# A two-layer encoder step on one core: residual stream kept feature by token, projections in split fp32r passes

## The chip, the core and the metric

The kernel runs on one core of one Trainium2 chip. The metric is device time in microseconds (us), as the median of the runs shown. Engines are named as in the profile: PE multiplies matrices (PEld is its loading of weights), DVE, ACT and POOL are the vector, scalar and GpSimd engines, SP issues loads from memory. PSUM is the banked memory into which PE adds up products.

## What is computed

320 tokens (256 of a prompt, 64 of running streams; in tiles of 128, 128 and 64) go through two layers of width 1024. The reference, cut to what matters:

```python
xn = rmsnorm(x, g_mix)
qa, ka, va, ga, ra, bb, cb, hb, qc, kc, vc = split_cols(xn @ w_in)
lg = jax.nn.log_sigmoid(ga @ w_g2 + b_g2) / GATE_TAU
o_a, s1 = gla_recurrence(s0, q, k, v, lg)
y_a = rmsnorm(o_a, g_gla) * jax.nn.silu(ra)
y_b, buf1 = short_conv(bb, cb, hb, w_conv, buf0)
o_c = diff_prompt(qd, kd, vd, lam)
y_c = rmsnorm(o_c, g_sub) * (1.0 - lam_init)
x = x + jnp.concatenate([y_a, y_b, y_c], axis=-1) @ w_out
x = x + ffn(rmsnorm(x, g_ffn))
```

w_in has 3088 columns: qa and ka 192 each, va, ra, qc, kc and vc 384 each, ga 16, bb, cb and hb 256 each. qd and kd are qc and kc after a norm per head and the rotary turn (rope). The ffn is dense SwiGLU (width 2816) in layer 0 and the top 2 of 8 SwiGLU experts (width 3584) in layer 1. Everything is fp32 in and out.

## The kernel before

Each engine runs one list of instructions, written out by hand, and waits on semaphores; the order on each engine is the order of the code. Weights come through a ring of three slots of 2 MB, filled by SP in the order of `UNITS`. PSUM banks are rings with a list of jobs each (A two banks, D three, S two, O one); a job can start when the job that had its bank before is read out.

One layer is mixed like this. x lies in rows, token by feature. `norm_tile` (L1473): ACT squares a tile, POOL takes the root, DVE scales it (L1001), PE transposes it (L1450), and ACT or DVE copies it with the gain into `xT`. Then PE projects. `tokens` and `token_tile` (L1508, L1500) make rows of qk, kc, qc, vc, va and ra, three token tiles of 384 columns each, as plain fp32 matmuls with `xT` as the stationary operand; `features` (L1493) makes ga and the blocks of bb, cb and hb feature by token. All matmuls are recorded at the helper `mm` (L1447), all transposes at `tr` (L1450). Gate logits go through DVE (L1050), the decays through ACT and DVE (L750 to L752, L1052 to L1061), rope through DVE (L1037 and L1080 to L1083), `heads_T` turns q and k, and ACT copies them. A loop over 12 heads (three tiles of four heads) follows, with the rest of the projections, the recurrence and the attention woven in. `project` (L1711) multiplies the mixed rows by w_out, in fp32, first the gated rows (three blocks of 128 features), then the convolution and the attention.

The dense FFN works otherwise: `CUTS` are pieces of 128 weight columns (8 x 128 x 128), each split by ACT into a high part in fp32r (`cut_hi`, L885) and by DVE into the rest (`cut_lo`, L1277), three cuts deep; `three` (L1751) multiplies in three fp32r passes: high by high, low weight by high x, high weight by low x. The experts work the same way on pieces of 2048 elements per partition (`split_hi` L916, `split_lo` L1351; matmuls L1869 to L1880).

Of the kernel before, what the change touches and what calls it, by code (L numbers as in the profile page):

```python
# [15 lines left out]
F32 = mybir.dt.float32  # L17
FR = mybir.dt.float32r
# [7 lines left out]
P = 128  # L26
# [38 lines left out]

RING = 3
SLOT = KB * 512
# [3 lines left out]
for _l in range(DEPTH):  # L71
    UNITS += [("qk", _l), ("kc", _l), ("qc", _l), ("vc", _l), ("va", _l), ("ra", _l), ("bc", _l), ("hb", _l),
              ("wo", _l, 0), ("wo", _l, 1)]
    if _l == 0:
        for _j in range((FB + 3) // 4):
            UNITS += [("g", _j), ("u", _j)]
        UNITS += [("d", _c, _j) for _c in range(2) for _j in range((FB + 7) // 8)]
UNIT = {u: n for n, u in enumerate(UNITS)}


def is_dense(u):
    return u[0] in ("g", "u", "d")


def plain_units(n):

    return sum(not is_dense(u) for u in UNITS[:n])

CUT = KB * P
CUTS = []
for _f in range(FB):
    CUTS += [(("g", _f // 4), "g", _f), (("u", _f // 4), "u", _f)]
for _c in range(2):
    CUTS += [(("d", _c, _m // 4), "d", (_c, _m)) for _m in range(FB // 2)]
CR = 3
LAST_CUT = {u: q for q, (u, _k, _w) in enumerate(CUTS)}
DOWN0 = 2 * FB  # L100
HALF = FB // 2
DOWN_BANKS = [[("A", 4 * _c), ("D", 4 * _c + 2), ("A", 4 * _c + 1), ("D", 4 * _c + 3)] for _c in range(2)]
UE = 3 * FC

PIECE = SLOT // 2
# [16 lines left out]
JOBS_A, JOBS_D, JOBS_S, JOBS_O = [], [], [], []  # L122


def _norm_jobs(i):
    for t in range(NT):
        JOBS_A.append(("xt", i, t))
        JOBS_D.append(("xt", i, t))


JOBS_A += [("par",), ("bcast", 0)]
JOBS_D += [("bcast", 1)]
for _l in range(DEPTH):
    _norm_jobs(2 * _l)
    JOBS_A += [("ga", _l)] + [("qk", _l, t) for t in range(NT)] + [("qkt", _l, t) for t in range(NT)]
    JOBS_A += [("pk", _l)] + [("kt", _l, t) for t in range(NT)] + [("vc", _l, t) for t in range(NT)]
    JOBS_A += [("qt", _l, t) for t in range(NT)] + [("va", _l, t) for t in range(NT)] + [("kd", _l, t) for t in range(NT)]
    JOBS_A += [("at", _l, 0), ("at", _l, 1), ("bb", _l, 0), ("at", _l, 2), ("bb", _l, 1), ("at", _l, 3), ("at", _l, 4)]
    JOBS_A += [("cb", _l, 0), ("at", _l, 5), ("cb", _l, 1)] + [("at", _l, n) for n in range(6, HEADS)]
    JOBS_A += [("ya", _l, t) for t in range(NT)] + [("wo", _l, 0), ("wo", _l, 1)]  # L140
    JOBS_D += [("gl", _l, 0), ("gl", _l, 1)]
    JOBS_D += [("kc", _l, t) for t in range(NT)] + [("qc", _l, t) for t in range(NT)]
    JOBS_D += [("ra", _l, 0), ("ra", _l, 1)] + [("att", _l, t) for t in range(NT)]
    JOBS_D += [("U", _l, 0), ("U", _l, 1), ("U", _l, 2), ("ra", _l, 2), ("U", _l, 3), ("U", _l, 4)]
    JOBS_D += [("oa", _l, t) for t in range(NT)] + [("hb", _l, 0), ("hb", _l, 1)]
    JOBS_D += [("wo", _l, t) for t in range(NT)]
    JOBS_S += [("s", _l, n) for n in range(HEADS)] + [("yc", _l, t) for t in range(NT)]
    JOBS_O += [("oc", _l, t) for t in range(NT)] + [("wo", _l, 2)]
    _norm_jobs(2 * _l + 1)
    if _l == 0:  # L150
        for _f in range(FB):
            JOBS_A.append(("g", _f))
            JOBS_D.append(("u", _f))
        JOBS_A += [("dT", _o) for _o in (0, 1, 4, 5)]
        JOBS_D += [("dT", _o) for _o in (2, 3, 6, 7)]
        for t in range(NT):
            JOBS_A.append(("dn", t))
            JOBS_D.append(("dn", t))
JOBS_D += [("lg", t) for t in range(NT)] + [("rk", t) for t in range(NT)] + [("cnt",), ("idx0",), ("idx",)]


class PsumRing:


    def __init__(self, banks, jobs, full, free):
        self.banks, self.full, self.free = banks, full, free
        self.n = {j: i for i, j in enumerate(jobs)}
        self.count = len(jobs)
# [36 lines left out]
def build(nc, A, O):  # L205
# [5 lines left out]
    with ExitStack() as ctx:  # L211
# [7 lines left out]
        A_full, A_free = sem("A_full"), sem("A_free")  # L219
        D_full, D_free = sem("D_full"), sem("D_free")  # L220
        S_full, S_free = sem("S_full"), sem("S_free")
        O_full, O_free = sem("O_full"), sem("O_free")
        RA_ = PsumRing(banks[0:2], JOBS_A, A_full, A_free)
        RO_ = PsumRing(banks[2:3], JOBS_O, O_full, O_free)

        RD_ = PsumRing([banks[3 + (i - len(JOBS_D) + 1) % 3] for i in range(3)], JOBS_D, D_full, D_free)
        RS_ = PsumRing(banks[6:8], JOBS_S, S_full, S_free)


        x = sb("x", [P, NT, D])  # L230
# [1718 lines left out]
```

## Time and profile before

| what | us |
|---|---|
| median of three runs (1794.09 to 1795.8) | 1794.45 |
| the profiled execution, own time | 1799.02 |
| its span on the core | 1797.2 |
| PE busy, of the span | 1705.6 (95%) |
| DVE busy | 1167.9 (65%) |
| ACT busy | 921.8 (51%) |
| POOL busy | 119.7 (7%) |

The profile is of one execution. The span is that of the core's instructions; the execution's own time is 1.8 us longer. Shares over the whole span mix stages: some 230 us of mixing a layer, 237 us of dense FFN, 976 us of experts. What holds a stage up is read from that stage.

### The profile page before, as it was taken

The numbers are of one execution on the slowest core, as the hardware profiler recorded it, in microseconds if no ns is written. First come the engines' busy times: TensorE is split into PE (matmuls) and PEld (weight loads), VectorE is DVE, ScalarE is ACT, GpSimd is POOL, SyncE is SP. The second block draws the span as 40 slices with busy tenths as digits, with TensorE's granted clock in tenths as the row PEclk, the third lists the DMA queues.
The fourth block names the chain that finished last, engine by engine and source line by source line (L and its number), as shares of the span: only waits on it lengthen the run. The fifth ranks groups of instructions, "written<-read, shape, count | busy, mean of one in ns | idle before, by whom it ended". The sixth has DMA issues, their size and how long they took to land.

```text
span 1797.2 us, 20002 instructions
## 1 busy us (share of the span) xinstructions
PE 1705.6 (95%) x7922; PEld 1305.3 (73%) x7922; DVE 1167.9 (65%) x1157; ACT 921.8 (51%) x975; POOL 119.7 (7%) x168
## 2 busy tenths in 40 slices
PE   5999979999999999879999999999999999999994
PEld 3456639999965566468878878888788788888883
DVE  2415524554325145168888888888888888888884
ACT  2312223333223112137777777777777777777772
POOL 4300200000012002010000000000000000000001
PEclk9999989999999989969999999999999999999997
DMA  5321227525413211079999999999999999999993
GB/s 171 101 97 47 97 103 272 184 75 200 141 58 116 82 48 51 29 286 363 360 368 379 368 372 369 358 386 365 359 386 361 370 377 359 378 373 358 385 365 100
DMA packets 202878, 450.02 MB, mean 250 GB/s; under 512 B 9634, under 2 KB 34928, under 8 KB 202784
## 3 DMA queue, kind: packets, MB, share of 16 engines
q1 hardware_dynamic: 187776, 420.63, 64.8%
q10 hardware_dynamic: 10944, 17.13, 2.7%
q0 software_dynamic: 4064, 10.96, 1.9%
q8 instruction: 64, 1.05, 0.2%
q14 instruction: 30, 0.25, 0.0%
HBM read 431.22 MB, written 17.47 MB: 250 GB/s over the span
## 4 chain that ended last, share of the span: by engine, by line
PE 90%; DVE 6%; ACT 2%; issue 1%; DMA 1%; ACTq 0%; POOL 0%; POOLq 0%; DVEq 0%
PE bank L1447 37%; PE bank L1869 12%; PE bank L1870 12%; PE bank L1871 12%; PE bank L1877 5%; PE bank L1880 5%; PE bank L1878 5%; PE bank L1450 2%; DVE split_lo L1351 2%; PE bank L1889 1%; DVE xgT_lo L1375 1%; ACT split_hi L916 1%; DMA raw<-expert_rows,pos 0%; DVE G L1342 0%; DVE xhat L1001 0%
## 5 line engine op out<-in xcount | busy, mean ns | idle before, releaser
L1351 DVE TENSOR_TENSOR split_lo<-raw,split_hi 128x2048 fp32r<-128x2048 f32 x336 | 768.2, 2291 | 133.7 <-ACT split_hi L916 133.7
L916 ACT CAST split_hi<-raw 128x2048 fp32r<-128x2048 f32 x336 | 641.2, 1913 | 268.9 <-PE bank L1871 169.0
L1869 PE MATMUL bank<-split_hi,xgT_hi 128*128 128x512 f32 x896 | 359.4, 401 | 6.0 <-DVE xgT_lo L1375 6.0
L1870 PE MATMUL bank<-split_lo,xgT_hi 128*128 128x512 f32 x896 | 355.8, 397 | 0.0
L1871 PE MATMUL bank<-split_hi,xgT_lo 128*128 128x512 f32 x896 | 355.7, 397 | 0.0
L1447 PE MATMUL bank<-ring,xT 128*128 128x384 f32 (+3 forms) x720 | 258.9, 516 | 5.3 <-DVE t L1037 3.4
L1447 PEld LDWEIGHTS bank<-ring,xT 128*128 128x128 f32 (+1 forms) x720 | 123.1, 174 | 130.3 <-issue 83.4
L1869 PEld LDWEIGHTS bank<-split_hi,xgT_hi 128*128 128x128 f32 x896 | 169.3, 189 | 45.8 <-DVE xgT_lo L1375 6.4
L1871 PEld LDWEIGHTS bank<-split_hi,xgT_lo 128*128 128x128 f32 x896 | 169.1, 189 | 41.1
L1870 PEld LDWEIGHTS bank<-split_lo,xgT_hi 128*128 128x128 f32 x896 | 169.5, 189 | 39.3
L1877 PE MATMUL bank<-split_hi,hmT_hi 128*128 128x512 f32 x448 | 179.3, 400 | 3.0 <-DVE split_lo L1351 3.0
L1878 PE MATMUL bank<-split_lo,hmT_hi 128*128 128x512 f32 x448 | 175.8, 392 | 0.0
L1277 DVE TENSOR_TENSOR cut_lo<-ring,cut_hi 128x1024 fp32r<-128x1024 f32 x66 | 80.7, 1225 | 120.2 <-ACT cut_hi L885 120.2
L885 ACT CAST cut_hi<-ring 128x1024 fp32r<-128x1024 f32 x66 | 69.1, 1052 | 149.8 <-PE bank L1447 141.9
L1880 PE MATMUL bank<-split_hi,hmT_lo 128*128 128x512 f32 x448 | 139.6, 393 | 0.0
L1447 PE MATMUL bank<-xT_hi,cut_hi 128*128 128x320 f32 x352 | 109.7, 312 | 3.8 <-DVE cut_lo L1277 3.8
L1447 PE MATMUL bank<-xT_lo,cut_hi 128*128 128x320 f32 x352 | 111.5, 317 | 0.0
L1447 PE MATMUL bank<-xT_hi,cut_lo 128*128 128x320 f32 x352 | 110.9, 315 | 0.0
L1877 PEld LDWEIGHTS bank<-split_hi,hmT_hi 128*128 128x128 f32 x448 | 84.3, 188 | 24.7 <-issue 4.9
L1188 DVE TENSOR_REDUCE mx<-bank 128x2 f32<-128x256 f32 (+2 forms) x24 | 13.3, 555 | 133.7 <-PE bank L1447 133.5
L1880 PEld LDWEIGHTS bank<-split_hi,hmT_lo 128*128 128x128 f32 x448 | 84.1, 188 | 19.5
L1878 PEld LDWEIGHTS bank<-split_lo,hmT_hi 128*128 128x128 f32 x448 | 84.2, 188 | 17.6
(233 smaller groups left out, 1656.0 us busy)
## 6 DMA issues: line engine op xcount, KB each, us to landing
raw<-moe_w_gate SPq DMA_DIRECT2D x112, 1024.0 KB, 8.0
raw<-moe_w_up SPq DMA_DIRECT2D x112, 1024.0 KB, 7.6
raw<-moe_w_down SPq DMA_DIRECT2D x112, 1024.0 KB, 5.4
ring<-w_in SPq DMA_DIRECT2D x12, 1536.0 KB, 6.8
ring<-ffn_w_gate SPq DMA_DIRECT2D x5, 2048.0 KB, 9.6
ring<-ffn_w_up SPq DMA_DIRECT2D x5, 2048.0 KB, 7.8
ring<-w_out SPq DMA_DIRECT2D x4, 2048.0 KB, 8.4
expert_rows<-zeros ACTq DMA_DIRECT2D x1, 8192.0 KB, 27.2
```

The source lines that it names most:

```text
L885: nc.scalar.copy(split_cut(cut_hi, q), raw_cut(q)).then_inc(cut_hi_ready, 1)
L916: return nc.scalar.copy(split_hi[:, i % SR, :], raw[:, (i % PR) * PIECE:(i % PR + 1) * PIECE]).then_inc(hi_ready, 1)
L1277: V.tensor_tensor(split_cut(cut_lo, q), raw_cut(q), split_cut(cut_hi, q).bitcast(F32), ALU.subtract).then_inc(cut_lo_ready, 1)
L1351: V.tensor_tensor(split_lo[:, i % SR, :], raw[:, (i % PR) * PIECE:(i % PR + 1) * PIECE], split_hi[:, i % SR, :].bitcast(F32), ALU.subtract ...
L1447: return issue(TE.matmul(out, lhsT, rhs, start=start, stop=stop))
L1450: return issue(TE.transpose(out, in_, ident[0:rows, 0:rows]))
L1869: TE.matmul(o, xgT_hi[:, kk, :], hi[:, c], start=kk == 0, stop=False)
L1870: TE.matmul(o, xgT_hi[:, kk, :], lo[:, c], start=False, stop=False)
L1871: last = TE.matmul(o, xgT_lo[:, kk, :], hi[:, c], start=False, stop=kk == KB - 1)
L1877: TE.matmul(banks[6 + n][:], hmT_hi[:, b, :], hi[:, cs[n]], start=b == 0, stop=False)
L1878: TE.matmul(banks[6 + n][:], hmT_hi[:, b, :], lo[:, cs[n]], start=False, stop=False)
L1880: last = TE.matmul(banks[6 + n][:], hmT_lo[:, b, :], hi[:, cs[n]], start=False, stop=b == FEB - 1)
```

## The change

x is kept feature by token (`xR`, 8 blocks of 128 features by 320 tokens) from the start to the end of layer 1. ACT and DVE split a block, with the gain, into `xT_hi` and `xT_lo`; the norm's factor of each token is not multiplied in. It comes from the squares of the blocks (ACT), added up by POOL (`add_squares`), summed over features by PE (`square_sums`), rooted by POOL, put on a diagonal by DVE and spread over the partitions by PE (`spread_rstd`) into `Rb`. It is multiplied onto the results: by DVE with `Rb` where the result stays feature by token (`by_R`), by ACT with one factor per row where it is turned into rows (`rows_copy`).

All of w_in (25 cuts a layer, the gate's 16 columns carried in a gap of qa's first cut) and w_out (8 cuts a layer) go through `cut_hi`, `cut_lo` and three passes. kc, qc, vc and va come out feature by token, DVE copies them to `fT`, PE turns them (`rows_T`), and ACT copies them out. The ring's slots are 1 MB, a unit holds 128, 192 or 256 columns. The PSUM rings are now C, T and S with two banks each, O with one, and D with one (three before). The norm's transposes are left out; x is transposed 24 times at the start and back at the end. In the experts, the matmuls of a piece that need only its high part come first, and those with its low part last.

```diff
-SLOT = KB * 512
+SLOT = 2 * CUT
...
+            def add_squares(i, o):
+                pool.wait_ge(sqx_ready, KB * i + o + 1)
+                if o == 0:
+                    nc.gpsimd.tensor_copy(acc[:], sqx[:, 0]).then_inc(acc_ready, 1)
+                else:
+                    pool.wait_ge(acc_ready, KB * i + o)
+                    nc.gpsimd.tensor_tensor(acc[:], acc[:], sqx[:, o % 2], ALU.add).then_inc(acc_ready, 1)
...
+            def x_hi(i, o):
+                R, job = norm_end(i, o)
+                act.wait_ge(R.free, R.emptied(job))
+                nc.scalar.activation(xT_hi[:, o, :], xR[:, o, :], ACT.Copy, scale=gcol(i)[:, o:o + 1]).then_inc(xhi_ready, 1)
+            def x_square(i, o):
+                R, job = norm_end(i, o)
+                act.wait_ge(R.free, R.emptied(job))
+                if KB * i + o >= 2:
+                    act.wait_ge(acc_ready, KB * i + o - 1)
+                nc.scalar.activation(sqx[:, o % 2], xR[:, o, :], ACT.Square).then_inc(sqx_ready, 1)
...
+                def rows_copy(name, c, out):
+                    act.wait_ge(RT.full, RT.filled(("tok", name, l, c)))
+                    b = RT.bank(("tok", name, l, c))
...
+                        last = nc.scalar.activation(out[0:rows, t, P * c:P * c + P], b[0:rows, P * t:P * t + P], ACT.Copy, scale=rstd[0:rows, 2 * l, t:t + 1])
+                    last.then_inc(RT.free, 1)
...
+            def x_lo(i, o):
+                dve.wait_ge(xhi_ready, KB * i + o + 1)
+                V.scalar_tensor_tensor(out=xT_lo[:, o, :], in0=xR[:, o, :], scalar=gcol(i)[:, o:o + 1],
+                                       in1=xT_hi[:, o, :].bitcast(F32), op0=ALU.mult, op1=ALU.subtract).then_inc(xlo_ready, 1)
...
+                def to_rows(job):
+                    i = through.index(job)
+                    if i >= 2:
+                        dve.wait_ge(RT.full, RT.filled(("tok", through[i - 2][0], l, through[i - 2][2])))
+                    dve.wait_ge(RC.full, RC.filled(job))
+                    V.tensor_copy(fT[:, i % 2], RC.bank(job)[:, 0:T]).then_inc(RC.free, 1)
+                def by_R(job, out, R):
+                    dve.wait_ge(RC.full, RC.filled(job))
+                    V.tensor_tensor(out, RC.bank(job)[:, 0:T], R, ALU.mult).then_inc(RC.free, 1)
...
+            def three(q, out, k, a, hi, lo, start, stop):
+                w_hi, w_lo = split_cut(cut_hi, q)[:, k, a:a + P], split_cut(cut_lo, q)[:, k, a:a + P]
+                mm(out, w_hi, hi, start, False)
+                mm(out, w_lo, hi, False, False)
+                return mm(out, w_hi, lo, False, stop)
+            def features(R, job, norm=None):
+                q = QN[job]
+                pe.wait_ge(cut_lo_ready, q + 1)
+                b = R.begin(pe, job)[:, 0:T]
+                for k in range(KB):
+                    if norm is not None:
+                        pe.wait_ge(xlo_ready, KB * norm + k + 1)
+                    last = three(q, b, k, 0, xT_hi[:, k, :], xT_lo[:, k, :], k == 0, k == KB - 1)
+                last.then_inc(R.full, 1)
...
+            def square_sums(i):
+                b = RD.begin(pe, ("ss", i))
+                pe.wait_ge(acc_ready, KB * (i + 1))
+                for t, (t0, rows) in enumerate(TILES):
+                    last = mm(b[0:rows, t:t + 1], acc[:, t0:t0 + rows], C("ones")[:, 0:1], True, True)
+                last.then_inc(RD.full, 1)
...
+            def spread_rstd(i):
+                b = RD.begin(pe, ("R", i))
+                pe.wait_ge(diag_ready, i + 1)
+                for t, (t0, rows) in enumerate(TILES):
+                    last = mm(b[:, t0:t0 + rows], C("ones", rows), diag[0:rows, t0:t0 + rows], True, True)
+                last.then_inc(RD.full, 1)
```

The order of a layer on PE, and the experts' piece, of the gate and up matrices:

```diff
+                features(RC, ("kc", l, 0), 2 * l)
+                square_sums(2 * l)
+                features(RC, ("kc", l, 1))
+                rows_T("kc", 0)
+                features(RC, ("kc", l, 2))
+                rows_T("kc", 1)
+                spread_rstd(2 * l)
+                features(RC, ("qc", l, 0))
...
+                features(RC, ("qa", l, 1))
...
+                gate_logits(0)
+                features(RC, ("ka", l, 0))
+                gate_logits(1)
+                features(RC, ("ka", l, 1))
...
+                features(RC, ("vc", l, 0))
+                features(RC, ("vc", l, 1))
+                rows_T("vc", 0)
...
+                rows_T("vc", 2)
...
-                    pe.wait_ge(lo_ready, ip * (2 * NP) + (i + 1 + PR))
+                    pe.wait_ge(hi_ready, ip * (2 * NP) + (i + 1))
...
-                            TE.matmul(o, xgT_hi[:, kk, :], lo[:, c], start=False, stop=False)
-                            last = TE.matmul(o, xgT_lo[:, kk, :], hi[:, c], start=False, stop=kk == KB - 1)
+                            TE.matmul(o, xgT_lo[:, kk, :], hi[:, c], start=False, stop=False)
+                        pe.wait_ge(lo_ready, ip * (2 * NP) + (i + 1 + PR))
...
+                            last = TE.matmul(o, xgT_hi[:, kk, :], lo[:, 512 * k:512 * k + 512], start=False, stop=kk == KB - 1)
```

Three places where the written order moves. The first is DVE from the gate logits on (`gla<-bank,pcol` reads the logits out of PSUM). Before:

```order
L1010 TENSOR_TENSOR xT<-bank,pcol 128x4x128 x2
L1010 TENSOR_TENSOR xT<-bank,pcol 128x4x64
L1050 TENSOR_SCALAR gla<-bank,pcol 128x320 x2
L1052 TENSOR_SCALAR gla<-gla 128x640
L1055 TENSOR_TENSOR gla<-gla 128x640
L1057 SCALAR_TENSOR_TENSOR gla<-const_sb,gla 128x320 x2
L1059 TENSOR_TENSOR gla<-gla 128x640
L1061 TENSOR_TENSOR gla<-gla 128x640
```

Now, from the second rope tile of k; `gla<-bank,Rb` scales ka's first cut:

```order
L1159 TENSOR_TENSOR t<-qkT,small_rs 128x384
L1214 TENSOR_TENSOR t<-t,CG 128x384
L1215 TENSOR_TENSOR t<-t,SG 128x8x24
L1216 TENSOR_TENSOR t<-t,SG 128x8x24
L1217 TENSOR_TENSOR xhat<-t 128x8x48
L1197 TENSOR_TENSOR gla<-bank,Rb 128x320
L1103 TENSOR_TENSOR cut_lo<-ring,cut_hi 128x1024
L1223 TENSOR_SCALAR gla<-bank,pcol 128x320
```

The logits stood ahead of the decays and all of rope; they now stand behind a rope tile, a scaling that reads a cut of PE, and a low part.

The second is ACT round the copies of q and k for the heads (`over` and `qkT` are their turned forms, L796 to L799 and L871 to L874 the exponentials of the decays). Before:

```order
L796 ACT_TABLE_LOAD
L796 ACTIVATE gla<-gla 128x640
L797 ACTIVATE gla<-gla 128x640
L798 ACTIVATE gla<-gla 128x640
L799 ACTIVATE gla<-gla 128x640
L762 ACTIVATE sq<-bank 128x384 x2
L762 ACTIVATE sq<-bank 64x384
L739 COPY pkT<-bank 128x512
L739 COPY over<-bank 128x4x128 x2
L739 COPY over<-bank 128x4x64
```

Now:

```order
L871 ACT_TABLE_LOAD
L871 ACTIVATE gla<-gla 128x640
L872 ACTIVATE gla<-gla 128x640
L873 ACTIVATE gla<-gla 128x640
L874 ACTIVATE gla<-gla 128x640
L757 CAST cut_hi<-ring 128x1024
L803 ACTIVATE vc<-bank,rstd 128x128 x2
L803 ACTIVATE vc<-bank,rstd 64x128
L814 COPY qkT<-bank 128x4x128 x2
L814 COPY qkT<-bank 128x4x64
```

Between the exponentials and the copies of q there are now the high part of a cut and the copies of vc's second cut out of a bank of T, the ring that the transposes of q use next.

The third is PE at the end of mixing (`am` and `aT` are attention weights, `Ya` the gated rows, in `xhat`'s place after the change; `y_hi` and `y_lo` the split mixed rows). Before:

```order
L1450 MATMUL bank<-const_sb,am 128x64
L1450 MATMUL bank<-const_sb,am 64x64
L1450 MATMUL bank<-const_sb,Ya 128x128 x6
L1450 MATMUL bank<-const_sb,Ya 128x64 x3
L1447 MATMUL bank<-pv,aT 64x96
L1447 MATMUL bank<-over,aT 64x96
L1447 MATMUL bank<-pv,aT 64x96
L1447 MATMUL bank<-over,aT 64x96
L1447 MATMUL bank<-ring,xT 128x512 x12
L1447 MATMUL bank<-ring,xT 64x512 x6
```

Now:

```order
L1710 MATMUL bank<-const_sb,am 128x64
L1710 MATMUL bank<-const_sb,am 64x64
L1707 MATMUL bank<-pv,aT 64x96
L1707 MATMUL bank<-vc,aT 64x96
L1710 MATMUL bank<-const_sb,xhat 128x128 x6
L1707 MATMUL bank<-pv,aT 64x96
L1707 MATMUL bank<-vc,aT 64x96
L1710 MATMUL bank<-const_sb,xhat 128x64 x3
L1710 MATMUL bank<-const_sb,xhat 128x128 x6
L1707 MATMUL bank<-y_hi,cut_hi 128x320
L1707 MATMUL bank<-y_hi,cut_lo 128x320
L1707 MATMUL bank<-y_lo,cut_hi 128x320
```

The products with w_out followed the last attention products and read rows turned just before; now they read `y_hi` and `y_lo`, made by ACT and DVE from the turned rows, and the rows of both kinds are turned ahead of them.

## Rows read from the trace of the kernel before

**Rows 1.** Windows: us, PE, PEld, DVE, ACT, POOL busy (instructions), PEclk, DMA share, GB/s
```profile
26.00:249.00 223.00, 215.87 (x864) 119.16 (x863) 78.48 (x179) 45.62 (x133) 31.59 (x51) 0.98 0.24 81
...
271.00:508.00 237.00, 236.39 (x1584) 236.16 (x1584) 107.27 (x134) 75.69 (x89) 0.00 (x0) 0.99 0.49 172
508.00:519.40 11.40, 7.23 (x50) 5.95 (x49) 8.04 (x13) 7.41 (x20) 6.09 (x10) 0.82 0.08 20
519.40:753.00 233.60, 227.05 (x880) 124.02 (x880) 79.07 (x179) 48.30 (x136) 28.91 (x42) 0.95 0.17 58
753.00:794.00 41.00, 24.05 (x166) 21.42 (x165) 25.87 (x84) 10.97 (x22) 7.69 (x9) 0.56 0.77 270
794.00:1770.00 976.00, 972.91 (x4309) 786.01 (x4310) 841.19 (x521) 713.79 (x524) 21.37 (x14) 1.00 0.99 360
```

**Rows 2.** Chain of waits, layer 0: start us, us, what
```profile
26.72 22.23 PE bank L1447 x64
...
52.07 15.84 PE bank L1447 x48
...
210.64 17.02 PE bank L1447 x44
...
248.58 0.88 PE bank L1450 x8
249.46 7.02 PE bank L1447 x16
...
270.80 198.31 PE bank L1447 x1320
```

**Rows 3.** Timeline of PE, one conv block: start us, us, what
```profile
171.60 4.57 PE L1447 MATMUL bank<-xT,ring 128*128 128x320 f32 x16
```

**Rows 4.** Groups by form: line engine op tiles count, busy us, mean ns, idle before
```profile
L1277 DVE TENSOR_TENSOR cut_lo<-ring,cut_hi 128x1024 fp32r<-128x1024 f32 x66 | 80.7, 1225 | 120.2 <-ACT cut_hi L885 120.2
L885 ACT CAST cut_hi<-ring 128x1024 fp32r<-128x1024 f32 x66 | 69.1, 1052 | 149.8 <-PE bank L1447 141.9 <-DMA ring<-ffn_w_up 7.8
...
L1273 DVE COPY xT<-bank 128x320 f32<-128x320 f32 x4 | 2.0, 492 | 8.3 <-PE bank L1447 8.3
```

**Rows 5.** The same view for 25 to 75 us
```profile
L590 POOL TENSOR_TENSOR CG<-const_sb,bc 128x144 f32<-128x144 f32 x4 | 2.0, 497 | 0.0
...
L1057 DVE TENSOR_TENSOR_SCAN gla<-const_sb,gla 128x320 f32<-128x320 f32 x2 | 1.6, 824 | 0.1
...
L591 POOL TENSOR_TENSOR SG<-const_sb,bc 128x72 f32<-128x72 f32 x4 | 1.4, 340 | 0.0
...
L796 ACT ACT_TABLE_LOAD x1 | 1.3, 1283 | 0.0
...
L1037 DVE TENSOR_TENSOR t<-bank,small_rs 128x384 f32<-128x384 f32 x2 | 1.1, 548 | 0.0
...
L797 ACT ACTIVATE gla<-gla 128x640 f32<-128x640 f32 x1 | 0.7, 720 | 0.0
```

**Rows 6.** Waits of PE: total us, times, longest
```profile
PE bank L1877 <- DVE split_lo L1351: 3.0, 8, 0.4
PE bank L1450 <- ACT kdn L739: 2.6, 2, 1.3
```

**Rows 7.** Windows round clock falls, columns as in rows 1
```profile
262.00:276.00 14.00, 6.31 (x27) 6.16 (x28) 7.98 (x20) 6.50 (x19) 0.71 (x2) 0.50 0.94 330
...
137.00:139.00 2.00, 2.00 (x4) 1.01 (x3) 1.89 (x2) 0.00 (x0) 0.00 (x0) 0.50 0.00 0
```

**Rows 8.** DMA issues: queue, count, KB each, median us from issue to landing
```profile
ring<-w_in SPq DMA_DIRECT2D x12, 1536.0 KB, 6.8
...
ring<-w_in SPq DMA_DIRECT2D x2, 1024.0 KB, 5.3
```

More of the change, by code:

```diff
@@ L74 @@
     if _l == 0:
-        for _j in range((FB + 3) // 4):
+        for _j in range(HALF):
             UNITS += [("g", _j), ("u", _j)]
[L77 to L95, printed above, removed]
@@ L103 @@
+PIECE = 2048
 UE = 3 * FC
-PIECE = SLOT // 2
 NP = 2 * UE
@@ new lines, in _ @@
+            act.wait_ge(RT.full, RT.filled(("par",)))
+            nc.scalar.copy(pcol[:], RT.bank(("par",))[:, 0:48]).then_inc(RT.free, 1)
+            act.wait_ge(RT.full, RT.filled(("bcast", 0)))
+            nc.scalar.copy(bc[:, 0:480], RT.bank(("bcast", 0))[:, 0:480]).then_inc(RT.free, 1)
+            act.wait_ge(RT.free, 2)
+            for q in range(CR):
+                hi(q)
+            for o in range(KB):
+                x_hi(0, o)
+            for o in range(KB):
+                x_square(0, o)
@@ new lines, in diagonal, with R_copy @@
+            def diagonal(i):
+                dve.wait_ge(rstd_ready, 2 * i + 2)
+                for t, (t0, rows) in enumerate(TILES):
+                    last = V.tensor_scalar(diag[0:rows, t0:t0 + rows], ident[0:rows, 0:rows], rstd[0:rows, i, t:t + 1], None, ALU.mult)
+                last.then_inc(diag_ready, 1)
+            def R_copy(i):
+                dve.wait_ge(RD.full, RD.filled(("R", i)))
+                V.tensor_copy(Rb[:], RD.bank(("R", i))[:, 0:T]).then_inc(RD.free, 1)
+                dve.wait_ge(RD.free, RD.emptied(("R", i)))
@@ new lines, in _ @@
+            for t, (t0, rows) in enumerate(TILES):
+                dve.wait_ge(RC.full, RC.filled(("xk", t, 1)))
+                V.tensor_copy(x[0:rows, t, 512:1024], RC.bank(("xk", t, 1))[0:rows, :]).then_inc(RC.free, 1)
+            for t, (t0, rows) in enumerate(TILES):
+                s = rs_slot(1, "end", t)
+                dve.wait_ge(rs_ready, s + 1)
+                dve.wait_ge(RC.free, RC.emptied(("xk", t, 1)))
+                V.tensor_scalar(xhat[0:rows, t, :], x[0:rows, t, :], small_rs[0:rows, s, 0:1], None, ALU.mult).then_inc(xhat_ready, 1)
@@ new lines, in _, with x_rows @@
+                if l:
+                    def x_rows(R, t, half):
+                        t0, rows = TILES[t]
+                        Rx, job = norm_end(3, 4 * half + 3)
+                        pe.wait_ge(Rx.free, Rx.emptied(job))
+                        b = R.begin(pe, ("xk", t, half))
+                        for o in range(4):
+                            last = tr(b[0:rows, P * o:P * o + P], xR[:, 4 * half + o, t0:t0 + rows], P)
+                        last.then_inc(R.full, 1)
+                    x_rows(RS, 0, 0)
+                    x_rows(RS, 1, 0)
```

1628 lines of the change are left out of this document (873 added, 755 removed).

## The prediction

> **What bounds the kernel now.** The table by stage comes first [rows 1]. Its columns after the length are the busy time of PE, PEld, DVE, ACT and POOL; PEclk is the granted TensorE clock, 1.00 being 2.4 GHz and 0.50 being 1.2 GHz. In all four long stages PE is busy 96% or more: mixing of layer 0 (26 to 249), its dense FFN (271 to 508), mixing of layer 1 (519 to 753) and the experts (794 to 1770). DVE and ACT are busy 35% and 20% of the mixing stages, so there they have room. Between them lie the norms and the router (508 to 519, 753 to 794, and after the first mixing): PE partly idle, at a lower clock.
>
> The chain of waits [rows 2] says what PE does in mixing: three tiles of a 384-column plain fp32 projection take 15.84 us, the first such together with the gate projection 22.23 us. It passes six of those per layer. The output projection runs from 210.64 to the end of the piece at 249.46, some 43.4 us of fp32 without the short pieces between. One conv block, 128 features of all 320 tokens in fp32, takes 4.57 us [rows 3]. Against that the FFN does 66 cuts of 128 columns in three fp32r passes in 236.39 us of PE time [rows 1]: 24 matmuls of 320 columns are **3.58 us a cut**.
>
> **PE's work.** Removed per layer: 6 x 15.84 + 6.4 (gate: 22.23 − 15.84) + 6 x 4.57 (conv) + 43.4 (output) = 172 us, and some 4 us of transposes of the norm and of q and k (eight took 0.88 [rows 2]). Added per layer: 25 + 8 = 33 cuts x 3.58 = 118 us, and 12 x 3 transposes of fT with their weight loads, 4 to 5 us. Net −53 to −49 a layer; I carry −49, since fT's transposes are short and come in threes. If PE stayed 96% busy, that would be the gain twice over, with the gaps on top.
>
> **What comes to wait.** Every cut now asks ACT 1.05 us (high part) and DVE 1.23 us (low part) [rows 4], and what comes out feature by token and is wanted by rows asks a copy of 0.49 us on DVE, three transposes on PE and three scaled copies on ACT (an estimate of 0.9 us: one of 640 columns takes 0.72, and there are 384 columns in three). None of it is much, but the queues are in written order, and PE waits for particular entries. I walked the four queues through one layer with the durations of [rows 4, 5]:
>
> - Norm. PE waits before the sums of squares for POOL's eight additions of 128 x 320. No such operation is in the trace; a product of 144 elements on POOL takes 0.50 us and one of 72 takes 0.34 [rows 5], a straight line through both gives 0.88 us at 320. Bounds: 0.50 (no slope) and 1.1 (in proportion to 144). Eight take 7 us beside 3.58 us of matmul: PE idle 2 to 2.5 us, and about as much again for the root (POOL) and spreading it: about **5 us** a norm.
> - Gate logits. They share one PSUM bank (the D ring now holds one), so the second waits until DVE has read the first; DVE reads it behind one rope tile (three operations of 0.55 us and two of half the width, 2.3 us), the scaling of ka's first cut, which PE has only just finished then, and a low part: at least 2.8 us (scaling, low part, reading and the handovers), walked **4.7**.
> - Transposes of k: wait for ACT's copy of v behind two high parts and the logarithm with its table: **2**.
> - Transposes of q: need the bank of v's second cut. DVE does the last rope tile (2.3), then the decays (4.1: two scans of 0.82 and three more of 640 columns); ACT then loads a table (1.28) and does four exponentials of 0.72, then a high part and the copy. In a row 2.3 + 4.1 + 4.2 + 1.05 + 0.9 = 12.5 us, of which PE has a few to fill: at least 7.7, walked **10.5**.
> - Decay transposes in head 2 wait for ACT's copy of va behind that head's exponentials: **4.5**.
> - Tail. Behind the last conv cut DVE has some 30 operations, 16.5 us (most of 320 to 384 columns and near 0.55 each), then ACT's high part of y (1.0) and DVE's low part (1.2) before the first output cut. Before, the output projection could begin with the gated rows alone (the piece at 210.64 [rows 2]), and the convolution hid under it. PE has about 5 us of small work left: **14** idle.
> - Clock. After waits of this size the clock falls. In the trace, PE between 137 and 139 stood at 0.50 soon behind a wait of 1.3 us for ACT's kdn [rows 6], and the matmuls from 262 to 276 all ran at 0.50 [rows 7]. A fall costs about 2 to 2.5 us of matmul here; three or four a layer beyond the present one or two: **8**.
>
> Sum of new waits: 5 + 4.7 + 2 + 10.5 + 4.5 + 14 + 8 = 49; gone are some 10 us of the present idle time and drops in mixing (7 us idle of 223 in [rows 1], the rest clock). So mixing gives back about 39 of the 49. It comes out at **some 220 us** a layer from first projection to the end of the output projection, where it was 229.8 in layer 0.
>
> **Stage by stage against the profiled span of 1797.2.**
> - Start and mixing of layer 0: the first projection begins at 26.7 now. The changed one begins sooner, but is paced by DVE, which copies and splits one feature block in about 1 us, so it is effectively under way at 30.6. End 249.5 instead of 256.5: **−7**.
> - Norm and FFN of layer 0: the cuts stay (66 of 3.58). Of the 14.3 us between output projection and first gate cut (256.48 to 270.80 [rows 2]) about 8 go, since blocks are normed while PE works; what stays is the residual sum and splitting of the last blocks and the sums of squares. DVE gains one more scaling per gate cut (0.5 us) but has room: 107 busy of 237 [rows 1]. **−8**.
> - Layer 1: the norm gap of 11 us goes under cuts, and 234 becomes 220: **−25**.
> - Norm and router: fewer steps, no second transposes; 40.7 becomes 34: **−7**. This is the least certain in proportion.
> - Experts: PE is busy 972.9 of 976 us; all that the new order can take is the wait for split_lo, 3.0 us in eight [rows 6]: **−3**. Another order of the same matmuls costs nothing by rows that alternate weights already.
> - DMA: cuts arrive in units of 1 MB or less, which landed in 5.3 us as a w_in unit of 256 columns, against 6.8 for 1.5 MB [rows 8]; the ring gives a unit about three and a half cuts, 12.6 us. **0**; below 0 there is nothing, as no matmul waited for it.
>
> Sum −50: span 1747, profiled execution 1749. That execution is 4.6 us above the median of the runs shown (1799.0 against 1794.45); the median forecast is **1745**. Bounds: with the waits at their least (7.7, 2.8, POOL at 0.50, tail half filled) 1722; with POOL at 1.1, every wait costing a clock fall and the router unmoved 1772.
>
> **Rivals.**
> - *PE stays the bound.* The cover I miss is there, and each layer gives the full 49: 1690 to 1700. For it: DVE and ACT are busy under 40% in mixing. Against: the waits for q and the tail are sums along one queue, not shares. Chance 0.09.
> - *Mixing gains nothing.* The queues are slower than walked (each wait delays the splitting of the next cuts as well, three cuts ahead at most), and only norms, router and experts give: −20 to −10, 1775 to 1785. For it: DVE gets some 4 us of entries per 3.58 us cut between the q and v cuts. Chance 0.13.
> - *Slower: the clock.* Before, long groups of fp32 kept PE at 0.95 to 0.98 in mixing [rows 1]; now PE works in pieces of 3.6 us with waits between. At 0.50, as from 262 to 276 [rows 7], a cut takes up to twice its 3.58 us: 118 us a layer if all were slow. It decides from about 26 us a layer, ten more falls of 2.5 us or over a fifth of the matmuls at 0.50: then 1800 or more, at half of them 1845. For: gaps of a few us are what the walk finds. Against: only six to eight of them. Chance 0.08. The Trainium skill, "TensorE: Matmul & The Clock Gate", section "HAM oscillation — how this bites in real kernels", says that waits between groups of matmuls let the clock fall again so that each group begins cold; by that rule this rival would be the likeliest, at 1800 or more. The rows agree that it falls behind a wait, and show that it recovers within a few us of dense work.
> - *The ring starves* in the parts with 128-column units: it needs landings over 12.6 us, and [rows 8] shows half that. Chance 0.03, 1770 to 1800.
>
> The forecast keeps 0.67. Its own bounds, 1722 to 1772, hold most of that; to leave out no more than 2 in 10 the range takes in part of both neighbours: **1708 to 1783**. A measurement of this kernel can tell about 0.2% (3.6 us). Slower by more: the clock 0.08 and a little of the starving ring, 0.09 together. Within 0.2%: 0.03, the upper end of the second rival. Faster: 0.88.
>
> **What would show it.** In the profile of the changed kernel: PE busy time down by about 100 us in all (−49 twice, some given back where the clock is lower), and PE's idle time up by 60 to 70; waits of PE for ACT's copies before the q transposes of about 10 us in each layer, for the logits' bank about 5, and one of 14 us before the first output cut; a granted clock of 0.90 to 0.95 in mixing; the experts' stage 976 us less the waits for split_lo; DVE's low parts 66 more and as long as now. It would be wrong in its main step if those waits are short (then under 1710), if the clock in mixing lies below 0.8, or if PE waits for landings.

## The result and the profile after

The changed kernel takes **1752.82 us** (median of four runs, 1752.47 to 1755.03), the kernel before 1794.29 beside it: a recorded ratio of 0.9759, 95% interval 0.9741 to 0.9776 (the quotient of the two medians, 0.9769, lies inside it). Forecast were 1745 and a range of 1708 to 1783. The profiled execution took 1753.11, its span 1751.2 against 1797.2.

The page of the changed kernel, its parts 1 and 2:

```profile
span 1751.2 us, 21767 instructions
...
PE 1626.5 (93%) x8526; PEld 1392.5 (80%) x8526; DVE 1291.2 (74%) x1346; ACT 987.4 (56%) x1042; POOL 144.7 (8%) x181
...
PEclk8988889999999797889999999999999999999997
```

PE's busy time fell by 79 us (1705.6 before), the span only by 46: PE stands 125 us of it, 33 more than before. The low digits of the clock lie in two groups of slices: the first mixing stage, and the second with the norm and router behind it.

The windows of the changed kernel by stage (columns as in [rows 1]), and below them three stretches of layer 0's mixing and one expert:

```profile
0.00:28.00 28.00, 16.73 (x50) 10.13 (x50) 9.95 (x20) 9.77 (x16) 9.38 (x21) 1.00 0.68 200
28.00:252.60 224.60, 187.19 (x1185) 167.24 (x1184) 136.60 (x264) 84.72 (x193) 51.99 (x70) 0.86 0.27 81
252.60:262.00 9.40, 4.99 (x33) 4.72 (x31) 4.92 (x8) 4.85 (x9) 4.11 (x4) 0.88 0.53 169
262.00:494.50 232.50, 232.12 (x1567) 231.67 (x1567) 132.33 (x190) 80.87 (x97) 8.39 (x12) 0.99 0.54 180
494.50:720.30 225.80, 192.30 (x1215) 173.07 (x1214) 132.41 (x257) 81.28 (x185) 34.44 (x41) 0.87 0.23 69
720.30:753.70 33.40, 19.62 (x168) 17.30 (x165) 26.30 (x84) 11.89 (x19) 8.98 (x13) 0.61 0.76 277
753.70:1729.00 975.30, 973.53 (x4320) 788.34 (x4320) 841.04 (x520) 713.85 (x526) 21.32 (x14) 1.00 0.99 363
...
102.00:116.00 14.00, 9.27 (x35) 8.09 (x36) 1.71 (x3) 6.62 (x14) 0.00 (x0) 0.53 0.34 110
204.00:221.20 17.20, 7.50 (x31) 4.72 (x31) 15.00 (x35) 4.42 (x15) 8.31 (x10) 0.53 0.02 2
221.20:225.40 4.20, 4.13 (x15) 4.17 (x16) 2.63 (x5) 0.85 (x3) 1.21 (x2) 0.50 0.00 0
1121.99:1243.40 121.41, 121.41 (x542) 98.37 (x541) 105.83 (x64) 89.76 (x67) 3.03 (x2) 1.00 1.02 373
```

Against [rows 1], the mixing stages are where the kernel has turned: PE is busy 83% and 85% of them instead of 97%, and its clock is 0.86 and 0.87 instead of 0.98 and 0.95. With the stages cut at the same events in both traces:

| stage | before | after | measured | forecast |
|---|---|---|---|---|
| start and mixing, layer 0 | 256.5 | 252.6 | −3.9 | −7 |
| norm and FFN | 251.5 | 241.9 | −9.6 | −8 |
| norm and mixing, layer 1 | 245.4 | 225.8 | −19.6 | −25 |
| norm and router | 40.7 | 33.4 | −7.3 | −7 |
| experts to the end | 1003.1 | 997.5 | −5.6 | −3 |

PE's waits in the changed kernel (engine, line, what it waited for: us in all, times, longest):

```profile
PE bank L1710 <- ACT vc L803: 19.0, 4, 8.4
PE bank L1707 <- POOL acc L598: 17.1, 3, 8.0
PE bank L1710 <- DVE am L1424: 12.5, 4, 3.4
PE bank L1710 <- DMA gla<-b_g: 9.9, 1, 9.9
PE bank L1707 <- DVE gla L1223: 7.9, 2, 4.0
PE bank L1710 <- DVE gla L1460: 6.4, 2, 3.2
PE bank L1710 <- ACT va L803: 6.2, 2, 3.1
...
PE bank L1707 <- DVE y_lo L1465: 2.7, 2, 1.3
```

These are the places of the walk, and within a layer they stand in its order of size: vc holds the transposes of k (1.2 in layer 0, 2.3 in layer 1) and of q (8.4 and 7.0), acc the sums of squares, `gla L1223` the second gate logits, va the decay transposes, and am, `gla L1460` and y_lo the tail. The 9.9 for b_g is the load of constants at the very start. The wait for split_lo [rows 6] is gone.

How the longest of them comes about, the chain of waits of the changed kernel (start us, us, what) shows:

```profile
97.95 0.84 DVE gla L1228
...
101.27 0.83 DVE gla L1234
...
102.76 0.72 ACT gla L872
...
104.73 0.93 ACT cut_hi L757
105.67 0.78 ACT vc L803 x3
...
106.58 1.10 PE bank L1710 x4
```

Decays on DVE, exponentials on ACT, one high part, the copy of vc, and only then PE's transposes of q: from 97.9 to 106.6 DVE is busy for 5.4 us and ACT for 4.5, so neither is short of time, but these pieces of work stand one behind another.

**Where mixing's gain went.** I cut the two mixing stages (475.2 us before, with the norm of layer 1; 450.4 after) into short slices and multiplied PE's busy time in each by 1 − PEclk: that is matmul time spent on the lower clock level. Before: 17 us idle, 18 lost to the clock, 440 of work at full clock. After: 71, 44 and 336. So the work shrank by 52 us a layer, and the layer gave back 27 in standing and 13 in clock. The parts of the change in mixing, the split passes and the other layout of x, were not run apart: that the work shrank is read from the two traces.

### The profile page after: what moved, and what is told of

Same layout as the page of the kernel before. It is cut to its first block, busy times and chain, and to the rows that moved or that the text cites. A ratio compares the mean times of both kernels' runs of the same rounds, so it can differ in the third digit from the quotient of the medians.

```text
span 1751.2 us, 21767 instructions
## 1 busy us (share of the span) xinstructions
PE 1626.5 (93%) x8526; PEld 1392.5 (80%) x8526; DVE 1291.2 (74%) x1346; ACT 987.4 (56%) x1042; POOL 144.7 (8%) x181
## 4 chain that ended last, share of the span: by engine, by line
PE 84%; DVE 9%; ACT 3%; issue 1%; DMA 1%; POOL 1%; POOLq 0%; ACTq 0%; SPq 0%; DVEq 0%
PE bank L1707 27%; PE bank L2128 12%; PE bank L2127 12%; PE bank L2132 12%; PE bank L2138 6%; PE bank L2147 6%; PE bank L2141 6%; DVE cut_lo L1103 2%; PE bank L1710 1%; ACT cut_hi L757 1%; PE bank L2156 1%; POOL acc L598 1%; DVE G L1610 0%; DMA xhat<-x_sample 0%; DVE t L1159 0%
## 5 line engine op out<-in xcount | busy, mean ns | idle before, releaser
L757 ACT CAST cut_hi<-ring 128x1024 fp32r<-128x1024 f32 x124 | 129.1, 1046 | 274.8 <-PE bank L1707 266.1
L1707 PE MATMUL bank<-xT_hi,cut_hi 128*128 128x320 f32 x752 | 250.0, 332 | 0.5 <-DVE xT_lo L1117 0.5
L2132 PE MATMUL bank<-split_lo,xgT_hi 128*128 128x512 f32 x896 | 246.3, 397 | 0.0
L1707 PE MATMUL bank<-xT_hi,cut_lo 128*128 128x320 f32 x752 | 243.1, 323 | 0.0
L1707 PE MATMUL bank<-xT_lo,cut_hi 128*128 128x320 f32 x752 | 242.9, 323 | 0.0
L1103 DVE TENSOR_TENSOR cut_lo<-ring,cut_hi 128x1024 fp32r<-128x1024 f32 x124 | 152.6, 1235 | 115.4 <-ACT cut_hi L757 115.1
L1707 PEld LDWEIGHTS bank<-xT_hi,cut_hi 128*128 128x128 f32 x752 | 151.3, 201 | 6.0 <-issue 3.0
L1707 PEld LDWEIGHTS bank<-xT_lo,cut_hi 128*128 128x128 f32 x752 | 152.5, 203 | 0.0
L1707 PEld LDWEIGHTS bank<-xT_hi,cut_lo 128*128 128x128 f32 x752 | 152.1, 202 | 0.0
L2147 PE MATMUL bank<-split_lo,hmT_hi 128*128 128x512 f32 x448 | 121.8, 393 | 0.0
```

The lines of the kernel that those rows point to most:

```text
L757: nc.scalar.copy(split_cut(cut_hi, q), raw_cut(q)).then_inc(cut_hi_ready, 1)
L1103: V.tensor_tensor(split_cut(cut_lo, q), raw_cut(q), split_cut(cut_hi, q).bitcast(F32), ALU.subtract).then_inc(cut_lo_ready, 1)
L1707: return TE.matmul(out, lhsT, rhs, start=start, stop=stop)
L2132: last = TE.matmul(o, xgT_hi[:, kk, :], lo[:, 512 * k:512 * k + 512], start=False, stop=kk == KB - 1)
L2147: last = TE.matmul(banks[6 + n][:], hmT_hi[:, b, :], lo[:, c], start=False, stop=b == FEB - 1)
```

## The experiments

The theory: mixing is set by the order of the entries on DVE, ACT and POOL, not by their load; each wait can be taken away by another order alone, and the clock comes back with it. The rivals: the waits move elsewhere when one goes, since the queues are full (then single edits give nothing and the sum falls short); or it is the clock that costs, and waits by themselves little. Each edit below is made to the changed kernel unless said otherwise, and spans are set against its 1751.2. The intervals of the ratios are some 4 us to either side: a gain of 7 us is just beyond them, one of 14 or 20 well beyond. The kernel before took 1793.6 beside e1 to e4, 1797.6 beside e5 to e7 and 1794.4 beside e8 and e9, so a comparison across these groups is rougher by some 3 us. Where a gain is split between PE's standing and the clock below, it is counted in both mixing stages together, cut at the same events and in slices as above. Line numbers shift by up to 11 between these kernels.

**e1_experts.** The kernel before with the experts' order alone (high-part matmuls first, the wait for the low part behind them):

```diff
-                    pe.wait_ge(lo_ready, ip * (2 * NP) + (i + 1 + PR))
+                    pe.wait_ge(hi_ready, ip * (2 * NP) + (i + 1))
...
+                        pe.wait_ge(lo_ready, ip * (2 * NP) + (i + 1 + PR))
```

> The kernel before with one part of the change: in the experts, matmuls that need only the high part come first, and the wait for the low part stands behind them. Waits theory: it takes the 3.0 us that PE waited for split_lo, 1791 us, and nothing else. Rival (the order itself matters, for instance because two passes in a row now use other weights): 1785 to 1800 by a changed time per piece, seen as another PE busy time than 972.9 us in the experts' stage. In the changed kernel the stages from the first expert on took 997.5 us instead of 1003.1, so 5.6 us is what this part should give if it explains that stage.

Measured: 1789.13, ratio 0.9966 (0.9953 to 0.998), 4.4 us below the kernel before beside it. One expert in windows, first of the kernel before:

```profile
1026.18:1148.26 122.08, 121.67 (x542) 98.32 (x541) 105.78 (x65) 89.91 (x67) 3.04 (x3) 1.00 1.01 370
```

then of this one:

```profile
1160.61:1282.00 121.39, 121.39 (x542) 98.39 (x541) 105.78 (x64) 89.92 (x67) 3.04 (x2) 1.00 1.01 372
```

The wait of 0.41 us in an expert is gone, and PE's busy time for the same 542 matmuls is 0.28 shorter too, which I had costed at nothing: 0.69 times 8 is 5.5 us, the −5.6 of the stage table. Why the busy time fell is open.

**e2_norm.** ACT squares a block two behind its high part, and PE sums one cut later (shown for the norm of layer 0; the two others are changed likewise):

```diff
-            for o in range(KB):
-                x_hi(0, o)
-            for o in range(KB):
-                x_square(0, o)
+            x_hi(0, 0)
+            x_hi(0, 1)
+            for o in range(KB):
+                x_square(0, o)
+                if o + 2 < KB:
+                    x_hi(0, o + 2)
...
-                square_sums(2 * l)
                 features(RC, ("kc", l, 1))
+                square_sums(2 * l)
```

> The changed kernel, with ACT's squares put between its high parts of x (two blocks behind) and PE's sums of squares one cut later, in all three norms by feature. Waits theory: the three waits for POOL (8.0, 4.4 and 4.7 us) go, with a clock fall of 2 to 2.5 us behind each: 1752.8 less 17 to 24, 1729 to 1736. Rival, queues are short of throughput: what PE does not wait there it waits at the next low part or copy, and under 5 us are left, 1748 to 1752.

Measured: 1733.03, ratio 0.966 (0.9636 to 0.9684); the span is 19.9 us shorter than the changed kernel's. All three waits for POOL (17.1 us) are gone; one of 2.6 us for the scaled gate is new, and those for vc went from 19.0 to 20.5. In the mixing stages PE stands 10.0 us less and loses 9.9 less to the clock. In the changed kernel POOL had stood, as its timeline shows (start us, us, instruction, idle before and its releaser):

```profile
28.11 1.53 POOL L595 COPY acc<-sqx 128x320 f32<-128x320 f32 x1 [17.52 <-ACT sqx L771]
29.79 7.01 POOL L598 TENSOR_TENSOR acc<-acc,sqx 128x320 f32<-128x320 f32 x7
```

Seven additions take 7.01 us, 0.88 each and the rest handovers between them, as estimated. What the prediction had missed is their start: ACT's list had all eight high parts ahead of the first square.

**e3_gl.** The second gate logits behind ka's second cut:

```diff
-                gate_logits(1)
                 features(RC, ("ka", l, 1))
+                gate_logits(1)
```

> The changed kernel with the second gate logits on PE one cut later, behind ka's second cut. Waits theory: the two waits of 4.0 us for DVE's reading of the bank go, with a clock fall each: 8 to 13 us, 1740 to 1745. Rival, DVE is short of throughput there (rope, low parts and copies, some 4 us per cut): the chain of DVE that follows ends no sooner, PE waits as much longer before q's transposes, and the time stays at 1750 to 1753.

Measured: 1739.86, ratio 0.9699 (0.9675 to 0.9723), span −13.8. The waits for the logits went from 7.9 to 0.9, and those for vc from 19.0 to 20.6. In the mixing stages PE stands 5.4 us less, and the clock gives back another 7.3: more than the standing itself.

**e4_vq.** The decays and their exponentials behind the copies of vc and q on both engines:

```diff
-                decays()
                 to_rows(("vc", l, 2))
                 lo(q0 + 15)
+                decays()
...
                 rows_copy("vc", 2, vc)
+                act.wait_ge(d_ready, 2 * l + 2)
+                nc.scalar.activation(eq, d1, ACT.Exp, scale=1.0 / 16)
```

> The changed kernel with the decays behind vc's last copy and low part on DVE, and ACT's exponentials of the decays behind the copies of q, so that neither stands between vc's second cut and the transposes of q; in the head loop DVE multiplies by the decays behind the first head's maximum. Waits theory: the two waits of 8.4 us shrink to 1 or 2, with one clock fall less each: 13 to 18 us, 1735 to 1740. Rival, the work only moves: ACT's exponentials then hold up the first heads, PE waits there for scores' banks or for the third cut of ra, and under 5 us are left, 1748 to 1752.

Measured: 1733.27, ratio 0.966 (0.9636 to 0.9685), span −19.6. The gain is a little above what was expected. The waits for vc go from 19.0 to 6.1 us; in the mixing stages PE stands 11.4 less and loses 7.3 less to the clock. Again more than the wait.

**e5_tail.** The convolution's, the gated rows' and attention's entries on DVE in another order, and one set of transposes behind the first output cut:

```diff
                     if n == 10:
                         sum_squares(l, "oa", 0, TILES[0][1], H)
+                        convolve(0)
...
-                transposed("yc", Yc, yc_ready, 1)
...
                 wo_cut(0, 0)
+                transposed("yc", Yc, yc_ready, 1)
```

> The changed kernel with the end of mixing reordered: on DVE the first convolution one head earlier, the gated rows, their turned product and the low part of the first three blocks ahead of the second convolution; on PE the transposes of attention's second tile behind the first output cut. Waits theory: of some 11 us that PE waits from the last head on, 4 to 6 a layer go, but the clock stays low there because the rest of the waits remain: 8 to 12 us, 1741 to 1745. Rival, DVE's total work after the last cut is what counts: the second output cut then waits for the convolution, and 0 to 3 us are left, 1750 to 1753.

Measured: 1746.44, ratio 0.9719 (0.9694 to 0.9744), span −7.4: between what the theory and the rival expected (the interval just touches the changed kernel's). PE's waits in the tail that are left:

```profile
PE bank L1711 <- DVE am L1424: 9.3, 4, 2.9
...
PE bank L1708 <- DVE y_lo L1461: 3.8, 2, 1.9
```

They were 21.6 us in the changed kernel and are 13.1: the two of 3.2 for `gla L1460` are gone, those for am go from 12.5 to 9.3, those for y_lo rise from 2.7 to 3.8. PE stands 8.0 us less in the mixing stages, the 4 a layer that were expected at the least, so here too another order takes waits away. The clock gives nothing back, 44.5 us lost against 43.9: with three waits of 1.8 to 2.9 us left in layer 0's tail, PE is on the lower level from 204.8 to 221.9 there (205.1 to 225.6 in the changed kernel). DVE is busy 15.0 of 17.2 us there (204.00:221.20 above); that order can't take away much more is argued from this, not shown.

**e6_all.** The four edits together (their diffs stand above).

> The changed kernel with the four edits together (norm, gate logits, decays, end of mixing). Waits theory: the gains add, as the waits lie in different places: 1752.8 less 19.8, 12.9, 19.5 (as measured one by one) and 10 for the end of mixing, 1690. Rival, they uncover a common limit (DVE's throughput in mixing): the sum falls short by a third or more, 1710 or above.

Measured: 1697.79, ratio 0.9443 (0.9419 to 0.9466), span −53.2 where the four alone make 60.7. By the medians it is 55.0 of 58.7, which is within the noise; the profiled execution was the slowest of the four. So neither the 1690 expected nor the rival's 1710 came: the 10 us expected of the tail were 6.4 alone, and nearly all of the rest adds up. Some of the shortfall is seen in this run's chain of waits:

```profile
229.66 11.19 DMA ring<-ffn_w_up
240.87 1.06 ACT cut_hi L757
...
244.24 5.88 PE bank L1718 x28
```

A load of 1 MB, 5.4 us in the median, took 11.19: it was issued 2.3 us behind the 8 MB of zeros for the experts' rows (227.33), where in the changed kernel the same load went out 1.8 us ahead of them and took 5.34. ACT waited 7.4 us for it, DVE for ACT, and PE stood for 2.6 until 244.24. In the mixing of layer 0 (28 to 224.75) PE is now busy 180.4 of 196.8 us, at a clock of 0.92.

**e7_warm.** No wait removed: idle matmuls (on operands already there, into a bank not yet in use) put into PE's waits for q and in the tail:

```diff
+                warm(("s", l, 0), 50)
                 for t in range(NT):
                     pe.wait_ge(rope_ready, 6 * l + 3 + t + 1)
...
+                        if m >= 10:
+                            warm(("wo", l, 0), 16)
...
+                warm(("wo", l, 0), 18)
                 transposed("ya", Ya, ya_ready, 2)
...
+                warm(("wo", l, 0), 7)
                 wo_cut(0, 0)
```

> The changed kernel with idle matmuls (a block of x times itself into a bank of S, result overwritten) put into PE's waits: 50 of them ahead of the transposes of q, and 16, 16, 18 and 7 at the four waits from the eleventh head's transposes to the first output cut, a little less time than PE waits there. No wait is removed. Clock theory: each fall of the clock costs matmul time behind its wait, so keeping PE busy gives back 2 to 2.5 us at q and 2 to 3 at the output cuts in each layer: 1742 to 1747. Rival, the falls cost nothing because the next wait takes up what a faster PE gains: 1751 to 1754. A third way, slower by the idle matmuls that overrun their wait: over 1755.

Measured: 1745.87, ratio 0.9711 (0.9683 to 0.9738), span −7.5, as expected. The tail in windows, before and from the first output cut:

```profile
204.00:218.20 14.20, 10.25 (x67) 8.25 (x66) 12.35 (x26) 2.93 (x10) 7.93 (x9) 1.00 0.02 1
218.20:222.40 4.20, 4.20 (x29) 4.20 (x30) 2.63 (x6) 0.75 (x3) 1.21 (x2) 1.00 0.00 0
```

The same stretch stood at 0.53 and 0.50 in the changed kernel. So it is the standing of PE that lowers the clock there, and matmuls that compute nothing hold it. But the matmul time lost to the clock falls by 17 us and the kernel by 7.5. Either a faster PE waits longer for DVE or ACT next, or idle matmuls overran their wait: they add 36 us of matmul time at full clock in the mixing stages, where PE stands 28 less. The two were not tried apart. The waits that got no idle matmuls, those for POOL, the logits and va, are unchanged at 17.1, 8.0 and 6.2.

**e8_fill.** e6 with the zeros issued later, in the middle of the FFN:

```diff
                         hi(G0 + 2 * f + 4)
+                        if f == 8:
+                            act.wait_ge(pool_zero, 6)
+                            act.dma_start(ybuf[NE * P:, :].rearrange("(p n) (c d) -> p (n c) d", p=P, c=4),
```

> The kernel of the four edits (e6_all, 1697.8, span 1698.0) with ACT's issue of the 8 MB of zeros moved from the start of the dense FFN to its ninth block. There, in e6_all, a weight unit issued at 229.66 landed only after 11.2 us, ACT's high part waited 7.4 us for it and PE stood still up to 244.24. Theory, the ring falls short beside the zeros once PE no longer waits for the norm: 4 to 6 us are won, part of what the four edits together fell short of the sum of the four alone (53.2 of 60.7 us of span): 1692 to 1694. Rival, the wait there is for DVE's scaling of the first gate cut, whose low parts come late anyway: 0 to 1 us, 1697.

Measured: 1690.52, ratio 0.9413 (0.9385 to 0.9442), 7.3 below e6, span −10.1; the kernel before stood 3.2 us lower beside it too and the two intervals overlap, so the size is rough. Of the 10.1, 3.5 lie in the mixing of layer 0, ahead of the place that was moved: the falls of the clock between 104 and 130 were shorter in this execution (0.87 on the mean from 110 to 130, 0.70 in e6). In the norm and FFN, where the edit is, 4.4 were won, as expected: PE stands 0.6 us there instead of 3.1, and the 1.7 that it lost to the clock are gone. The other 2.2 lie behind, in stages that the edit leaves alone; the mixing of layer 1 lost 14.1 us to the clock for 16.6. Beside the zeros loads are as slow as before (11.10 and 14.00 us), and ACT waits for the ring longer than in e6 (15.9 us in all against 10.6), but not PE.

**e9_best.** e8, with ACT's copies of va and kdn ahead of the exponentials of heads 1 to 3, and idle matmuls in the tail:

```diff
+                        if 1 <= n <= 3:
+                            rows_copy("va", n - 1, va)
...
+                            warm(("wo", l, 0), 16 if m == 10 else 12)
...
+                warm(("wo", l, 0), 10)
                 wo_cut(0, 0)
```

> As e8_fill, with ACT's copies of va and of the turned decays ahead of the exponentials in heads 1 to 3, and idle matmuls (16, 12 and 10) in PE's waits of the last heads and ahead of the first output cut, so that the clock stays up. Theory, the rest of mixing's loss is the copies' wait (3.1 us a layer) and clock falls there and at the first output cut (2 to 3 us each a layer): 8 to 12 us under e8_fill, 1682 to 1686. Rival, exponentials that come later hold up the heads' chain on DVE as much as the copies held up PE: 3 to 6 us, from the idle matmuls alone.

Measured: **1683.32**, ratio 0.9371 (0.9344 to 0.9399): the fastest of the study and where it was expected, though the 7.2 us below e8 are just short of the 8 to 12. Its mixing in windows (which reach 4.0 and 2.3 us into the next stages):

```profile
28.00:221.50 193.50, 184.17 (x1251) 165.55 (x1250) 141.88 (x271) 86.51 (x196) 49.31 (x68) 0.97 0.32 96
453.00:650.00 197.00, 186.74 (x1265) 168.05 (x1264) 134.17 (x260) 82.33 (x186) 35.13 (x41) 0.97 0.26 79
```

PE is busy 95% of both, some 7 us a layer of it with idle matmuls, and the clock is back at 0.97. Cut where the mixing ends, as in the changed kernel, the stages take 189.5 and 194.8 us, 35 and 31 less than there. PE's waits for va go from 6.2 in e8 to 1.5 and those for am from 9.8 to 1.4; what each of the two edits gave was not tried apart.

## Why the prediction was right, and where it was off

- **The direction and the bound.** PE's work fell by 52 us a layer at full clock, 49 were carried. That hides one term: fT's transposes, put at 4 to 5 us a layer, are 72 with 12.9 us of busy time, 6.4 a layer (some at the lower clock).
- **The waits.** Walked 40.7 us a layer without the clock, measured 32 to 36: logits 4.0 for 4.7, k 1.2 and 2.3 for 2, q 8.4 and 7.0 for 10.5, va 3.1 for 4.5, tail 10.8 for 14 (2.9 and 3.4 for am, 3.2 for `gla L1460`, 1.3 for y_lo). The norm alone was longer: 5 forecast, 2 to 2.5 of them before the sums; measured 8.0, 4.4 and 4.7 before the sums and nothing behind, since the root runs under two cuts. The addition's price was right, but 7 us beside 3.58 leave 3.4, not 2 to 2.5; and that ACT starts POOL late was overlooked, though it stands in ACT's written order.
- **The clock: the step that failed.** It was put at 8 us a layer, from falls of 2 to 2.5 us; in the two mixing stages it rose by 25.5, 12.8 a layer. The number of falls was right, three more a layer: the trace has 6 and 8 in the two stages, where there had been 3 and 5 and not one or two. Their size was not: 3.1 us of matmul each on the mean, 2.2 before. A fall behind a single wait cost 1.7 to 4.8 us (3.3 and 3.4 behind va's 3.1 us, 4.8 round q's 8.4, from 102 to 116), one with four waits close together 5.9 and 6.1 (the tail, 204 to 225 in layer 0). I read [rows 7] as one price for every fall, but falls run together where waits do. The clock of 0.90 to 0.95 forecast for mixing came to 0.86.
- **Idle time.** Forecast 60 to 70 more, measured 33 over the span, and PE's busy time fell by 79 instead of 100 (104 of work, less 25.5 of clock). The 60 to 70 did not follow from the forecast itself: a span 50 shorter with 100 less of busy time leaves 50 more idle, and less with the clock's share given back. The error of the waits and that of the clock have opposite signs, and the total is near the forecast partly for that.
- **Stages.** The norm and FFN and the router came within 2 us. Layer 1 gave 19.6 for 25, layer 0 3.9 for 7. The clock took 16.0 us more than before in layer 0 and 9.6 in layer 1, for the 8 put down: more than the whole shortfall of layer 0, and a part of layer 1's. The experts gave 5.6 for 3: e1 shows 0.28 us of busy time an expert that was costed at nothing.
- **The rivals.** "Slower by the clock" did not come: it needed 26 us a layer and got 12.8. The Trainium skill, "TensorE: Matmul & The Clock Gate", section "HAM oscillation — how this bites in real kernels", says that waits between groups of matmuls let the clock fall, so that each group begins cold. It holds here in its mechanism: e7 filled the waits of the tail and the clock stood at 1.00. Not in its extent: a mean of 0.86 leaves most of the matmuls at the full level. "PE stays the bound" (1690 to 1700) was no fact of the changed kernel, but e6 at 1697.79 and e8 at 1690.52 reach it with the same arithmetic: its cover existed, in the wrong order. "Mixing gains nothing" did not come, as the two mixing stages together became 24.8 us shorter; nor did the starving ring, as no wait of PE is for a landing in it.

That the waits are order and not load is shown by e2, e3 and e4, whose edits move entries and remove none; in the tail, with DVE near full, e5 shows it for 8.0 us of some 22. That a wait costs more than its length is shown by e2 to e4 too: with 10.0, 5.4 and 11.4 us of standing 9.9, 7.3 and 7.3 of clock came back. By e5 it is not so everywhere: 8.0 us of standing went there and the clock gave back nothing.

## What to carry to other kernels

When a faster arithmetic shortens the engine that bounds, walk the lists of the engines that feed it for entries nobody waits for yet that stand ahead of entries somebody does; a load of 40% says nothing of it. Price a wait together with the clock behind it, and price falls that follow each other as one long fall; such a fall can stay when only some of its waits go (e5). Idle matmuls in a wait that can't be moved are worth trying, but only after the order is right, since they give back less than the clock took.

## What the runs showed of the hardware

**POOL and DVE hold each other up.** In e2 POOL's additions run beside DVE's splitting of x; the timeline there:

```profile
23.71 0.54 DVE L1127 SCALAR_TENSOR_TENSOR xT_lo<-xR,pcol,xT_hi 128x320 fp32r<-128x320 f32 x1
23.97 8.22 POOL L598 TENSOR_TENSOR acc<-acc,sqx 128x320 f32<-128x320 f32 x7 [0.27 <-ACT sqx L771]
24.17 0.48 DVE L1120 COPY xR<-bank 128x320 f32<-128x320 f32 x1
24.57 0.76 DVE L1127 SCALAR_TENSOR_TENSOR xT_lo<-xR,pcol,xT_hi 128x320 fp32r<-128x320 f32 x1
...
29.57 1.89 DVE L1113 TENSOR_TENSOR cut_lo<-ring,cut_hi 128x1024 fp32r<-128x1024 f32 x1
```

The low part of x takes 0.54 us where it started ahead of the additions and 0.76 beside them, the low part of a cut 1.89 instead of 1.23 [rows 4], and seven additions 8.22 instead of 7.01; the copy out of PSUM stays at 0.48. The Trainium skill, "SBUF — State Buffer", section "Who interferes with whom", says that a DVE instruction with two inputs in SBUF contends with a GpSimd instruction that reads SBUF, and one with at most one such input, outside its two-port modes, does not; the rows agree on which instructions are slowed. It is seen from overlaps, no run was made for it alone.

**A large write slows loads on another queue.** Beside the 8 MB of zeros, which ACT issues, a 1 MB load issued by SP took 11.19 us instead of 5.4 (e6), and 11.10 in e8. **The same wait gives falls of different length.** Behind the same wait, 110 to 130 stood at 0.70 in e6 and 0.87 in e8, two programs that are alike up to there; so single executions differ by some 3 us from this alone.

**Not every fall of the clock has a wait just ahead of it.** In the changed kernel no wait of PE between 134 and 205 is longer than 0.3 us, and yet the clock falls (windows of that kernel):

```profile
162.00:164.00 2.00, 2.00 (x13) 1.58 (x11) 1.97 (x3) 0.41 (x1) 0.00 (x0) 1.00 0.00 0
164.00:166.00 2.00, 1.69 (x20) 1.15 (x20) 1.90 (x5) 0.63 (x1) 0.00 (x0) 1.00 0.00 0
166.00:168.00 2.00, 2.00 (x10) 1.51 (x11) 1.86 (x7) 0.78 (x3) 0.00 (x0) 0.89 0.37 26
168.00:170.00 2.00, 2.00 (x9) 2.00 (x9) 1.93 (x3) 1.26 (x5) 0.00 (x0) 0.50 0.85 325
```

This fall, from 167.6 to 171.0, cost 1.7 us of matmul. What brings it on is open.
